# GpSimd splits each weight chunk in six instructions in place of two

## The reference

```python
def first_block(x, ...):                 # layers 1 and 2 (A)
    for l in range(DEPTH):
        h = rms_norm(x, attn_norm[l])
        proj = h @ w_in[l]
        ...
        mixed = jnp.concatenate([out_a, out_b, out_c], axis=-1)
        x = x + mixed @ w_out[l]
        h = rms_norm(x, ffn_norm[l])
        x = x + (jax.nn.silu(h @ w_gate[l]) * (h @ w_up[l])) @ w_down[l]
...
def second_block(x, mem, ...):           # layers 3 (R) and 4 (F)
    for layer in range(DEPTH):
        h = rms_norm_2(x, norm_mix[layer])
        ...
        x = x + jnp.concatenate([y_mix, y_mem], axis=-1) @ w_out[layer]
        x = x + sqrelu_mlp(rms_norm_2(x, norm_mlp[layer]), w_mlp_in[layer], w_mlp_out[layer])
```

## Time and profile before

| | us |
|---|---|
| median of 3 runs | 2629.04 |
| lowest, highest | 2625.93, 2629.22 |
| the profiled execution, its own time | 2628.46 |
| its span in the profile | 2626.7 |
| TensorE busy | 2412.6 (92%) |
| VectorE busy | 1561.1 (59%) |
| GpSimd busy | 1492.4 (57%) |
| GpSimd, subtraction of a chunk (line 627), 194 times | 883.9 |
| GpSimd, rounding of a chunk (line 625), 194 times | 358.3 |
| ScalarE busy | 405.9 (15%) |

### The profile page before, as it was taken

One profiled execution on the slowest core, in us unless ns is written; L12 is line 12 of the kernel. 1 busy time (PEld: TensorE's weight loads), 2 busy tenths in 40 slices (PEclk: granted clock), 3 DMA queues, 4 the chain that ended last, 5 costly groups with the idle time before them and its releaser, 6 DMA issues.

```text
span 2626.7 us, 28227 instructions
## 1 busy us (share of the span) xinstructions
PE 2412.6 (92%) x10786; PEld 1935.4 (74%) x10786; DVE 1561.1 (59%) x1482; ACT 405.9 (15%) x688; POOL 1492.4 (57%) x656
## 2 busy tenths in 40 slices
PE   5978899999997889999997689999999898999999
PEld 4666678888766668888876457788887775787887
DVE  7786676653578656665358667507666463771450
ACT  3222111110122311111000411001111132110000
POOL 3355566656646566665664465566654555565664
PEclk9988899999998899999998799999999988999999
DMA  3210122222311012222232112222232200222222
GB/s 137 70 56 1 64 81 96 96 87 99 110 62 55 1 64 97 96 96 82 99 123 73 40 64 96 80 96 96 96 112 80 81 17 16 81 97 95 96 96 80
DMA packets 37838, 207.86 MB, mean 79 GB/s; under 512 B 3532, under 2 KB 10316, under 8 KB 16888
## 3 DMA queue, kind: packets, MB, share of 16 engines
q1 hardware_dynamic: 37752, 206.70, 22.6%
HBM read 204.55 MB, written 2.13 MB: 79 GB/s over the span
## 4 chain that ended last, share of the span: by engine, by line
PE 47%; DVE 15%; ACT 2%; issue 2%; POOL 1%; DVEq 0%; ACTq 0%; POOLq 0%
PE ps L801 13%; PE ps L806 13%; PE ps L805 13%; DVE act L1637 3%; DVE ssq L1637 2%; DVE t L1645 2%; DVE h L1645 1%; PE ps L1162 1%; DVE nt L1645 1%; DVE nt L1637 1%; DVE t L1637 1%; ACT act L1310 1%; PE ps L1136 1%; PE ps L874 1%; DVE x L1637 1%
## 5 line engine op out<-in xcount | busy, mean ns | idle before, releaser
L627 POOL TENSOR_TENSOR wl<-raw,wh 128x2048 fp32r<-128x2048 f32 (+1 forms) x194 | 883.9, 4556 | 16.2
L625 POOL TENSOR_SCALAR wh<-raw 128x2048 fp32r<-128x2048 f32 (+1 forms) x194 | 358.3, 1847 | 855.7 <-PE ps L801 663.3
L801 PE MATMUL ps<-h,wh 128*128 128x512 f32 x1576 | 623.6, 396 | 41.7 <-DVE x L1637 11.4
L805 PE MATMUL ps<-h,wh 128*128 128x512 f32 x1576 | 618.2, 392 | 0.0
L806 PE MATMUL ps<-h,wl 128*128 128x512 f32 x1576 | 618.2, 392 | 0.0
L801 PE MATMUL ps<-act,wh 128*128 128x512 f32 x1120 | 442.4, 395 | 26.2 <-DVE x L1637 17.1
L805 PE MATMUL ps<-act,wh 128*128 128x512 f32 x1120 | 439.6, 393 | 0.0
L806 PE MATMUL ps<-act,wl 128*128 128x512 f32 x1120 | 439.4, 392 | 0.0
L801 PEld LDWEIGHTS ps<-h,wh 128*128 128x128 f32 x1576 | 298.8, 190 | 117.8 <-issue 34.3
L806 PEld LDWEIGHTS ps<-h,wl 128*128 128x128 f32 x1576 | 298.8, 190 | 63.0
L805 PEld LDWEIGHTS ps<-h,wh 128*128 128x128 f32 x1576 | 299.1, 190 | 62.0 <-issue 1.0
(11 more groups left out here) (339 smaller groups left out, 2870.6 us busy)
## 6 DMA issues: line engine op xcount, KB each, us to landing
raw<-w_gu SPq DMA_DIRECT2D x44, 1024.0 KB, 4.8
raw<-w_up SPq DMA_DIRECT2D x32, 1024.0 KB, 4.8
raw<-w_down_b SPq DMA_DIRECT2D x32, 1024.0 KB, 4.8
raw<-w_down_a SPq DMA_DIRECT2D x32, 704.0 KB, 4.1
raw<-w_in_a SPq DMA_DIRECT2D x14, 1024.0 KB, 4.9
raw<-w_in_f SPq DMA_DIRECT2D x13, 1024.0 KB, 4.9
raw<-w_in_r SPq DMA_DIRECT2D x11, 1024.0 KB, 4.9
raw<-w_out_a SPq DMA_DIRECT2D x8, 1024.0 KB, 7.7
```

What stands on the lines that cost most here:

```text
L625: pool.tensor_scalar(hi_s, raw[s][:, 0:n], 1.0, 1.0, ALU.mult, ALU.mult).then_inc(hi_done, 1)
L627: pool.tensor_tensor(lo_s, raw[s][:, 0:n], hi_s.bitcast(F32), ALU.subtract).then_inc(w_ready, 1)
L801: first = pe.matmul(out, w_hi, v_hi, start=start, stop=False)
L805: pe.matmul(out, w_hi, v_lo, start=False, stop=False)
```

## The change

In `split`, the rounding of a chunk is issued in two halves of the columns (1024 each, 704 in `w_down_a`) one behind the other, and the subtraction in four quarters (512, or 352). The first quarter waits until the first half is rounded, the third until the second is; `hi_done` counts up to five per chunk in place of one. `w_ready` is raised by the last quarter, as before by the one subtraction. Buffers, transfers, and the programs of the other engines stay as they are.

```diff
-                pool.tensor_scalar(hi_s, raw[s][:, 0:n], 1.0, 1.0, ALU.mult, ALU.mult).then_inc(hi_done, 1)
-                pool.wait_ge(hi_done, hi.up())
-                pool.tensor_tensor(lo_s, raw[s][:, 0:n], hi_s.bitcast(F32), ALU.subtract).then_inc(w_ready, 1)
+                halves = (slice(0, n // 2), slice(n // 2, n))
+                for part in halves:
+                    pool.tensor_scalar(hi_s[:, part], raw[s][:, part], 1.0, 1.0, ALU.mult, ALU.mult).then_inc(hi_done, 1)
+                    hi.up()
+                for j in range(4):
+                    if j % 2 == 0:
+                        pool.wait_ge(hi_done, hi.at(j // 2 - 1))
+                    part = slice(j * n // 4, (j + 1) * n // 4)
+                    ins = pool.tensor_tensor(lo_s[:, part], raw[s][:, part], hi_s[:, part].bitcast(F32), ALU.subtract)
+                    if j < 3:
+                        ins.then_inc(hi_done, 1)
+                hi.up(3)
+                ins.then_inc(w_ready, 1)
                 split_out.up()
```

## The result

The changed kernel takes 2570.67 us (median of 4 runs, 2565.82 to 2573.60), the kernel before 2629.13 beside it (4 runs, 2625.93 to 2631.09): a ratio of 0.9773, 95% interval 0.9760 to 0.9787. The forecast was 2588 with a range from 2570 to 2614. The sign and the mechanism were right, but 58.5 us came back where 41 were forecast. The profiled span fell by 60.1 us, from 2626.7 to 2566.6, where the sum had 40.4. The largest miss is term (5), the input projections.

What follows compares the result with a forecast made beforehand. TensorE, busy 2412.6 of 2626.7 us, was the bound; its 214 idle us and the clock behind pauses could be won. Seven terms, six gains and +4.9 of costs, summed to -40.4 us: 2628.5 to 2588 us, range 2570 to 2614.

Steps and rivals of the forecast that it cites:

- the mechanism: A VectorE operation on SBUF operands stands until GpSimd's instruction ends; shorter pieces cut that wait, and TensorE's pauses with it.
- term (5): Input projections, VectorE full: only PSUM operations in between help; layer 3 -3.0, layer 4 -2.5, layers 1 and 2 -0.7: -6.2 us (0 to -12).
- Term (1): Four output projections: eight TensorE pauses, 20.9 us, shrink to about 1.0 us a stage, less the late second chunk: -14.1 us.
- Term (2): Up to down in layers 3 and 4: four pauses, 8.3 us, go, and clock lost behind them returns: -13.9 us.
- Term (3): Clock behind the output projections' pauses: 1.7 us lost at three of them; booked -2.5 us (0 to -5.1).
- term (4): Memory keys of layer 3: small operations lose 10.4 us to two chunks, TensorE pauses 8.11; after, six lose about 1.0 each: -4.2 us.
- Term (6): Chunk amid windowed attention, two layers: `sm` takes 3.90 us, TensorE pauses 2.49 behind it: -4.4 us; layer 3's attention no gain.
- term (7): Costs: +3.4 us for three late input chunks, +1.5 for later copies in layers 3 and 4's attention: +4.9 us.
- hold on in pairs: Rival: GpSimd goes straight on between pieces that wait for nothing, VectorE loses up to 2.4 us: -20 us, 2608; chance 0.13.
- The kept loss: Rival: every operation meets a piece's start, VectorE loses 5.8 us a chunk as now: -3.7, 2625, no change; chance 0.06.
- GpSimd as the bound: Rival: pieces cost more, GpSimd bounds 1408-column chunks and layers 3 and 4; at 0.5 us more a piece 2684 us; chance 0.06.
- More comes back: Rival: 3 us of layer 3's 9 us attention pause, output-projection clock and input projections in full: 2572 us; chance 0.08.

Runs made afterwards that it cites:

- the two runs above: The change with twelve-piece chunks in input projections 3 and 4 and layer 3's attention chunk whole, then layer 4's whole too: 2562.57 and 2561.87 us.
- twelve pieces: Every chunk in four roundings of 512 and eight subtractions of 256 columns, against the kernel before: 2585.76 us, ratio 0.9833.

## Where the prediction was right, and the steps that failed

**What bounds the kernel, and the mechanism: right.** A VectorE operation on SBUF waits out the GpSimd instruction it meets, and nothing else of the kernel had to change. `h<-x,vec,h` fell to 1.34 us and `act<-nt,act` to 1.63 (forecast: under 1.8), the subtractions take 1.45 us (1.3 to 1.6), no pause behind `x` is over 1.05 us but for the 5.6, none is left behind `act`, the clock from up to down is 1.00, and waits for the split are 18.2 us (16 to 18). Where VectorE had been in nobody's way (the feed-forward of layers 1 and 2) nothing was won.

**Term (1), pauses of the output projections: right in mechanism and nearly in size.** Of the eight pauses of 20.9 us there stays 1.05 us in each of the four stages (forecast 1.0), and the late second chunks went from 0.27 to 0.46, 0.70 and 0.72 us, in place of +0.95 each: -15.6 us, not -14.1. A row costs VectorE 3.57 + 1.25 = 4.8 us (forecast 5.0).

**Term (2): right**, 14.5 us against 13.9.

**Term (3), the clock behind these pauses: mis-sized.** The stages give 21.2 us, of which (1) explains 15.6 and the 5.74 us pause that is now 5.58 another 0.2: 5.4 us are clock, where I booked 2.5 and had 5.1 as the bound. "The pauses don't vanish wholly" was the wrong reason: in the 10 us behind each pause of 1.05 us that stays, the granted clock is 1.00. Nor does the length of a pause tell it: before the change, 1.84, 2.14 and 3.16 us (298.77, 330.02, 948.59) were followed by 10 us at 0.83 to 0.84, and 2.14, 3.18, 2.67, 3.13 and 2.63 us (979.77, 1554.25, 1584.41, 2236.79, 2266.91) by 10 us at 1.00.

**Term (5), input projections: this step failed.** It had 6.2 us. The stages gained 18.6; less the 4.4 of term (4), and with the 2.8 that later splits cost there, some 17 us are left for it, beyond its bound of 12. "After, six operations in close order lose 6 x 0.96 = 5.8 ... so nothing is won where VectorE is full" holds three errors. The 0.96 is the price behind a subtraction of 512; behind a rounding of 1024 it is 0.7 (1.41 for an operation of 0.69 to 0.75 alone). In general an operation that stands in line from the start of a piece loses the piece plus 0.35 less its own 0.69, since GpSimd pays only 0.35 us for letting it in: each handover lets about half of it run beside GpSimd. By that, a VectorE that is always full loses 1.59 + 4.26 = 5.9 us to a whole chunk, 2 x 0.70 + 4 x 0.93 = 5.1 to the change's and 4 x 0.25 + 8 x 0.35 = 3.8 to one in twelve. Measured in layer 3's input projection, the loss fell by 1.5 and 3.1 us, against 0.8 and 2.1 so. The second error is the rest: VectorE there isn't full of SBUF operations, and each handover more lets it reach its next PSUM operation, which runs beside a piece (the run with the rounding alone cut shows this: 1.1 us a chunk, where the prices give 0.2). The third is the clock: in layer 3's stage TensorE is busy 92.80 us before and 90.22 after, for the same 416 matmuls, 2.6 of the 8.5 us. In layer 1 the step had 0.7 for two layers and the trace shows 4.9 in the first. TensorE starts 1.83 us later (26.59), and yet the pause of 3.39 us of the earlier trace rows is 0.74:

```profile
26.59 0.76 PE L811 MATMUL ps<-h,wh 128*128 128x512 f32 x1 [9.22 <-POOL wl L633]
33.22 0.50 PE L811 MATMUL ps<-h,wh 128*128 128x512 f32 x1 [0.74 <-DVE h L1655]
```

Before, ahead of the pause, behind it, and where the pace changes:

```profile
27.88 0.63 PE L805 MATMUL ps<-h,wh 128*128 128x512 f32 x1
28.30 0.63 PE L806 MATMUL ps<-h,wl 128*128 128x512 f32 x1
...
32.91 0.63 PE L805 MATMUL ps<-h,wh 128*128 128x512 f32 x1
33.34 0.63 PE L806 MATMUL ps<-h,wl 128*128 128x512 f32 x1
...
37.30 0.40 PE L805 MATMUL ps<-h,wh 128*128 128x512 f32 x1
37.53 0.39 PE L806 MATMUL ps<-h,wl 128*128 128x512 f32 x1
```

From the first tile at 24.76 on, these start 0.43 to 0.59 us apart, on both sides of the pause, about twice the 0.23 from 37.30 on. After, only the first seven do, up to 29.7 us; before, it was nineteen. The spacing is that of half clock. The clock column reads 1.00 all through, but it can't speak here: the trace has no record of the clock ahead of 37.1 us (29.8 after), and a stretch without one is printed as 1.00. So the pause didn't bring the slow pace, which was there from the start; before, it lasted on behind the pause, and after, it was over ahead of it. After, TensorE is busy 51.44 us for 210 matmuls (26 to 81 us), before 54.07 for 209 (24 to 85). I had used that pause as a cover for a cost and not asked what work at half pace stood around it.

**Term (4), memory keys:** the pause of 8.11 us became 3.67, that is -4.4 (forecast -4.2).

**Term (6), the windowed attention: the gain came, but not as I said.** The pause of 2.49 us behind `sm` is still 2.45. It only comes earlier, since `sm` isn't blocked and the pause ahead of it fell from 2.01 to 1.15 us. Of the 9.3 us in layers 1 and 2 (forecast 4.4), 4.1 are clock (4.3 in layer 1, -0.2 in layer 2): from 180 to 195 it is granted at 0.77 before, and at 1.00 in the stretch that answers to it after. The rest is idle time, 1.4 us in layer 1 and 3.9 in layer 2. As the two runs above show, the part in clock is partly luck, and with this chunk alone in pieces the two layers gained 4.4 us; the trace of one run can't price it. "No gain booked" for layer 3's attention was short of a cost: 3.6 us were lost again there, where term (7) had 1.5 for layers 3 and 4 together, and the margin of 0.6 us that I had read said that GpSimd's later copies would show.

**Term (7), costs: too high for a chunk.** I put five gaps of 0.08 us into a chunk and an intercept of the line through 512 columns; the pieces follow each other without gaps, and a chunk grew by 0.43 us in place of 1.0. At twelve pieces the split at 179.25 in that run ends 7.88 us later, +1.27. So one instruction more costs GpSimd 0.11 to 0.13 us. The prediction counted three late input chunks and overlooked a fourth, at 1434.51 us; the four waits grew by 2.8 us together (it had 3.4 for three). That left the 1408-column chunks and those of layers 3 and 4 clear of the bound, as said.

**The rivals.** The pieces don't hold on in pairs: every handover in the rows above is behind a single piece. The kept loss is out: the pauses behind `x` went. GpSimd as the bound isn't there at six pieces and is at twelve, and then in the input projections of layers 1 and 2, which I hadn't looked at, and not in the feed-forward. "More comes back", 2572 with a chance of 0.08, was the nearest, but its own terms don't add up to that: 3 us, 2.6 more of (3) and 5.8 more of (5) make 2577, so that it comes near by a slip in the sum. It named two of the sources, (3) and (5), and put the third in layer 3's 9 us pause, which grew from 9.12 to 9.96 us.

## What to carry to other kernels

When one engine blocks another for the length of an instruction, price an operation by what is left of the instruction that it meets, and look at which operation stands in line when the longest one begins; a cut pays by letting work that isn't blocked come in between. Cut only as far as the blocking engine has time in that stage: the same pieces won 18 us in one input projection, and in another 10 went behind a wait of 1.5. And ask of every TensorE pause what clock stands behind it: here that was over a third of the gain (21.5 of 60.1 us). Give it a range, since pauses of one length were followed by either clock.

## What the runs showed of the hardware that I had not expected

- GpSimd pays some 0.12 us for one instruction more in a row (6.61 us for a chunk in two instructions, 7.04 in six, 7.88 in twelve), and 0.35 to 0.45 for letting a VectorE operation of 0.69 us in.
- A pause of 1.5 us of TensorE in a stretch of 128-column matmuls was followed by 20 us at 0.50 while TensorE was busy 4.00 of every 4.00 us; behind 1.05 us in a stretch of 512-column ones nothing was lost, and before the change five pauses of 2.14 to 3.18 us in such stretches were followed by 10 us at 1.00, three of 1.84 to 3.16 us by 0.83 to 0.84.
- The same instructions with the same pause of 2.44 us were granted 1.00 in one kernel and 0.78 in another. The two traces of that stage differ by 5 us, and so much is uncertain in one profile of it.
